# Hybrid decoder trunk: order of the fourth head's products and split of the last head's gating in the matrix-memory layer

## The reference

```
s   = (q k^T) * exp(d - m)                  # scores times decays
num = w_inter * (q C) + s v                 # per head, 256 value features
qn  = w_inter * (q n) + sum(s)
h   = num / max(|qn|, exp(-m))
C   = w_old * C + sum(w_s * k v^T)          # the state, carried from block to block
y   = (sigmoid(o) * h) @ w_out              # gate, then the output product
```

## Time and profile before

| what | value |
|---|---|
| median of 3 runs | 1314.68 us |
| the profiled execution | 1314.32 us |
| its span (first to last instruction) | 1312.5 us |
| outside the span | 1.8 us |
| granted TensorE clock, mean | 0.999 |
| busy: PE, DVE, ACT, POOL | 99%, 65%, 44%, 5% |
| recurrence and start of the output product | about 171 to 206 us of the span |

### The profile page before, as it was taken

How to read it: one execution, slowest core, us unless ns; L and a number is a source line. 1 busy time by engine, 2 the same in 40 slices (tenths; PEclk the granted TensorE clock), 3 DMA queues, 4 the chain that set the end, 5 groups by cost and what they waited for, 6 DMA issues and landing times.

```text
span 1312.5 us, 25501 instructions
## 1 busy us (share of the span) xinstructions
PE 1304.9 (99%) x10940; PEld 1270.3 (97%) x10940; DVE 856.1 (65%) x1554; ACT 583.2 (44%) x1033; POOL 68.0 (5%) x104
## 2 busy tenths in 40 slices
PE   9999999999999999999999999999999999999998
PEld 8999989999999999999999987999999999999998
DVE  6437676887777775222887788698777777432385
ACT  5222354654444443222755768554444444322371
POOL 1110331000000000000012010000000000000000
PEclk9999999999999999999999999999999999999999
DMA  5543732223233234222414232221232233322231
GB/s 176 168 108 99 239 113 79 84 66 96 84 95 97 84 95 134 89 89 83 145 33 160 83 98 79 83 79 42 91 97 92 86 98 105 116 89 89 77 130 66
DMA packets 35089, 131.64 MB, mean 100 GB/s; under 512 B 4228, under 2 KB 4812, under 8 KB 34688
## 3 DMA queue, kind: packets, MB, share of 16 engines
q1 hardware_dynamic: 29520, 111.33, 26.5%
q0 software_dynamic: 5024, 18.05, 4.4%
q10 hardware_dynamic: 432, 0.64, 0.2%
HBM read 121.08 MB, written 10.05 MB: 100 GB/s over the span
## 4 chain that ended last, share of the span: by engine, by line
PE 96%; DVE 2%; ACT 2%; issue 0%; POOL 0%; DVEq 0%; ACTq 0%; POOLq 0%
PE tile L1159 24%; PE tile L1161 24%; PE tile L1163 24%; PE tile L1169 4%; PE tile L1170 4%; PE tile L1171 4%; PE tile L1674 1%; PE side L1169 1%; PE side L1170 1%; PE side L1171 1%; DVE wL L1857 0%; PE side L1289 0%; ACT xH L768 0%; PE side L1334 0%; ACT wH L741 0%
## 5 line engine op out<-in xcount | busy, mean ns | idle before, releaser
L741 ACT ACTIVATE wH<-raw 128x1024 fp32r<-128x1024 f32 (+1 forms) x190 | 210.7, 1112 | 381.1 <-DMA raw<-in_w_up 149.1
L1159 PE MATMUL tile<-xH,wH 128*128 128x260 f32 x1800 | 364.4, 283 | 0.0
L1163 PE MATMUL tile<-xH,wL 128*128 128x260 f32 x1800 | 362.7, 283 | 0.0
L1161 PE MATMUL tile<-xL,wH 128*128 128x260 f32 x1800 | 362.2, 283 | 0.0
L1857 DVE TENSOR_TENSOR wL<-raw,wH 128x1024 fp32r<-128x1024 f32 (+1 forms) x190 | 246.1, 1296 | 154.4 <-ACT wH L741 150.2
L1159 PEld LDWEIGHTS tile<-xH,wH 128*128 128x128 f32 x1800 | 277.3, 189 | 3.2 <-DVE kvq L1905 2.6
L1163 PEld LDWEIGHTS tile<-xH,wL 128*128 128x128 f32 x1800 | 277.5, 188 | 0.0
L1161 PEld LDWEIGHTS tile<-xL,wH 128*128 128x128 f32 x1800 | 276.8, 188 | 0.0
L1905 DVE SCALAR_TENSOR_TENSOR u<-tile,rstd 128x520 f32<-128x520 f32 x96 | 67.1, 699 | 122.8 <-PE tile L1163 122.7
L1159 PE MATMUL tile<-hidH,wH 128*128 128x260 f32 x616 | 124.3, 283 | 0.0
L1163 PE MATMUL tile<-hidH,wL 128*128 128x260 f32 x616 | 123.8, 282 | 0.0
(11 more groups left out here) (462 smaller groups left out, 1895.8 us busy)
## 6 DMA issues: line engine op xcount, KB each, us to landing
raw<-in_w_up SPq DMA_DIRECT2D x88, 512.0 KB, 3.6
raw<-in_w_down SPq DMA_DIRECT2D x32, 704.0 KB, 4.1
raw<-in_w_ple SPq DMA_DIRECT2D x16, 512.0 KB, 5.3
raw<-in_w_qo SPq DMA_DIRECT2D x12, 512.0 KB, 3.6
raw<-in_w_qkv SPq DMA_DIRECT2D x12, 512.0 KB, 3.6
raw<-in_w_kv SPq DMA_DIRECT2D x10, 512.0 KB, 3.6
cring<-in_c_in POOLq DMA_DIRECT2D x8, 512.0 KB, 4.5
out_c_s<-cring POOLq DMA_DIRECT2D x8, 512.0 KB, 3.6
```

The source lines that it names most:

```text
L741: nc.scalar.activation(wH[j][:, 0:n], raw[j][:, 0:n], ACT.Copy).then_inc(s_high, 1)
L1159: nc.tensor.matmul(out[:, q, 0:HT], wh, x[0][:, k, tokens(q)], start=first, stop=False)
L1161: nc.tensor.matmul(out[:, q, 0:HT], wh, x[1][:, k, tokens(q)], start=False, stop=False)
L1163: mm = nc.tensor.matmul(out[:, q, 0:HT], wl, x[0][:, k, tokens(q)], start=False, stop=last)
```

## The change

Three edits. PE does `scores(3)` ahead of `outer(1, 2, NB)` and `values(1)`, no longer behind them. The last of the last head's four numerators is divided by DVE (`last_numerator`), directly behind `denominators(3)`, instead of by ACT. `gated(3)` raises a semaphore of its own after its first half, on which ACT starts the first of the last head's two roundings, and it stands ahead of `clear_acc()`.

```diff
+        s_gated0 = sem("last_head_half_gated")
...
             def numerators(n):
-                for b in range(NB):
+                for b in range(NB - 1 if n == NH - 1 else NB):
...
             def x_high(n):
-                act.wait_ge(s_afin, n + 2)
+                if n == NH - 1:
+                    act.wait_ge(s_gated0, 1)
+                else:
+                    act.wait_ge(s_afin, n + 2)
                 for k in (2 * n, 2 * n + 1):
+                    if k == 2 * NH - 1:
+                        act.wait_ge(s_afin, NH + 1)
                     nc.scalar.activation(xH[:, k, :], o_tile(k), ACT.Copy).then_inc(s_xh, 1)
...
+            scores(3)
             outer(1, 2, NB)
             values(1)
-            scores(3)
             turn_numerators(0)
...
                     last = nc.vector.tensor_tensor(o, side[:, half, :], o, ALU.mult)
+                    if half == 0 and n == NH - 1:
+                        last.then_inc(s_gated0, 1)
                 last.then_inc(s_afin, 1)
+
+            def last_numerator():
+                n, b = NH - 1, NB - 1
+                at0 = NB * (n % 2) + b
+                dve.wait_ge(s_den, 2 * NH)
+                nc.vector.tensor_scalar(ytok[n % 2][:, b, :], num_bank(b)[:, 0:DV], rden[:, at0:at0 + 1], None, ALU.mult
+                                        ).then_inc(s_nr, 1)
...
             denominators(3)
+            last_numerator()
             low("mout", 2)
+            gated(3)
             clear_acc()
-            gated(3)
             dve.wait_ge(s_xr, XSET["mout"] + 2 * (NH - 1))
             o_low(NH - 1)
```

## The result

The changed kernel takes **1317.97 us** (median of 15 runs, 1316.30 to 1319.60), the kernel before beside it 1314.53 (15 runs, 1314.17 to 1315.36): a ratio of 1.0025 [1.0018, 1.0032] (the bracket is the 95% interval), 3.44 us **slower**. The prediction was 1314.2, no change, in a range that ended at 1315.0. It was wrong.

A forecast was written before the change was run, and what follows sets the result against it. PE, busy 99% of the span, bounds the kernel; only its idle time could be gained. Early gains were lost waiting for POOL's k = 5, leaving 0.48 us at k = 7: 1314.68 - 0.48 = 1314.2 us, range 1313.4 to 1315.0.

The forecast's parts named there:

- edit 2: Last numerator divided by DVE: `low` starts 0.49 later, `turn_numerators(3)` loads 0.82 earlier including the earlier gain of 0.45.
- rival 3: Slower: POOL runs k = 4 and k = 5 before `low`; PE's k = 7 1.3 late, 1316.0 us; chance 0.09.
- decision point: On DVE, `low` starts after POOL's k = 4 only if `last_numerator` takes over 0.6 us.
- edit 1: `scores(3)` moved ahead on PE: `outer(2, 0)` 0.50 earlier, 0.45 us taken as gained, bounds 0.28 and 0.50.
- the tight wait at `outer(2, 2)`: PE's `outer(2, 2)` needs ACT's numerators of head 1, ready at 187.44; up to 0.1 us given back.
- edit 3: Half gating, `clear_acc` later: memset falls inside the wait for POOL, semaphore costs nothing, k = 7 loads at 204.43.
- Rival 2: No gain: POOL's k = 4 first by a little, `low` waits, k = 7 0.1 later, 1314.8 us; chance 0.15.
- About 0.2% ... none of the cases reaches that: About 0.2%, or 2.6 us, is what measurement can tell from no change; no case was said to reach it.
- The four waits: PE's late starts at 181.45, 200.35, 204.36 and 204.91: 0.40, 0.46, 0.33 and 0.19 us, together about 1.3.

The follow-up runs named there:

- e2: Changed kernel with `scores(3)` back behind `values(1)`, so only the moved division, half gating and later memset remain: 1317.29 us against 1314.49 before.
- e4: Changed kernel with POOL's scaling of head 2's queries made to wait for the sample outputs' last step: 1316.69 us against 1314.49 before.
- e5: Changed kernel with 18 additional, unused matmuls on PE ahead of its wait for k = 6: 1316.14 us against 1314.62 before.
- e10: Changed kernel with a tiny DVE memset between `last_numerator` and `low`: 1317.80 us against 1314.47 before.
- e12: Changed kernel with a 4-column memset on POOL, and a wait for it, between k = 4 and k = 5: 1315.39 us against 1314.48 before.
- e11: Changed kernel with a 4-column memset on POOL, and a wait for it, ahead of k = 4: 1314.81 us against 1314.47 before.
- e9: Changed kernel with a 256-column memset on POOL, and a wait for it, ahead of k = 4: 1314.92 us against 1314.47 before.
- e1: Kernel before with only `scores(3)` moved ahead of `outer(1, 2, NB)`: 1314.70 us against 1314.49.
- e8: Kernel before with only half gating of the last head and `clear_acc()` behind `gated(3)`: 1314.12 us against 1314.62.
- e7: Kernel before with `clear_acc()` moved ahead of `low` on DVE: 1314.62 us against 1314.62.
- e6: Changed kernel with `low` moved into `states(1)` and POOL's scaling of head 2's queries behind the sample outputs: 1313.22 us against 1314.62 before.

## Why the prediction was wrong

**The step that failed most: edit 2, "`low` lies at 199.28 to 200.49".** All the working behind it took a lead of 0.17 over POOL for a won race. The lead came out as foreseen (0.15), and the race was lost, to both tiles. What happened is rival 3, to which 0.09 was given and which the range left out: POOL first with k = 4 and with k = 5, `low` after them, then `gated(3)`, `x_high` and k = 6 and 7. Its decision point ("if `last_numerator` takes over 0.6 us") was wrong: the new instruction took 0.48, inside its bounds, and was enough. Recorded leads in these runs, all with POOL's k = 4 as the other side: behind the division 0.15 to 0.17 lost (after, e2, e4, e5, e10, e12), 0.34 and 0.57 won (e11, e9); behind the reciprocal 0.66 to 0.70 won (before, e1, e8); behind the big memset 0.13 won (e7). Counting from the recorded end of DVE's instruction ahead of `low` sorts them no better: leads of 0.07 to 0.09 lost (after, e2, e4, e5, e10, e12), 0.05 won (e7). For a recorded lead within 0.2 us both outcomes should have had a fair chance, and 1316 should have been in the range.

The Trainium skill, "SBUF — State Buffer", section "SBUF: two separate sides", says that of a VectorE instruction with two SBUF inputs and a GpSimd instruction that reads SBUF, whichever starts first has the shared ports for its whole length; its section "Who interferes with whom" says: "Issue order, not op shape, decides who blocks." The runs agree on the holding: whichever lost ended 1.1 to 1.2 us after the other had (`low` in the changed kernel and e12, k = 4 in e7, e8 and e11), nearly its own length. They differ from the plain reading of it: the order of the starts in the trace is not that order, since `low`, recorded 0.15 earlier, lost.

**Rival 3's price was too small**: +1.3 at k = 7; it was +1.93. That miss is edit 1's, below: rival 3 counted on edit 1's 0.45, and where edit 1 does gain (e4), k = 7 is only 1.10 late. The larger miss is behind k = 7: PE's idle 2.05 us were followed by 3.3 us at 1.2 GHz, worth 1.4 to 1.8 (e5; 1.50 by the distances). No step of the prediction had the clock.

**Edit 1, "I take 0.45 gained", failed too.** It was a loss of 0.22 at `outer(2, 0)`. The prediction looked for waits behind the delayed instructions, but not at which of them meets POOL, and it counted the query scaling among the delayed, which it wasn't: the sample outputs' last step, delayed with the rest, came just behind the scaling and took 1.07 instead of 0.23. It also left out that `turn_numerators(0)` waits for that step. With that order put right (e4, e6) the gain is 0.55, close to the 0.50 that was worked out; the tight wait at `outer(2, 2)` cost nothing that shows.

**Right:** `low` holds POOL and the memset doesn't (e7, e8); k = 4 ends 1.17 after `low`; PE would wait some 0.8 at k = 5 if `low` were first (0.90 in e9 and e11); edit 3 costs nothing and gains by itself (0.38 at k = 7, e8). Rival 2 was the right kind of doubt (POOL "first by a little") with one tile too few. "About 0.2% ... none of the cases reaches that" fell with rival 3's price. The four waits that the prediction lists add up to 1.38 us, not 1.3; nothing hangs on it.

## What to carry to other kernels

Before delaying a VectorE instruction that reads two SBUF operands, list what GpSimd runs within a microsecond of it, and count a lead of a few tenths as a race that may be lost, to everything queued back to back on GpSimd. The cure here was not to make it faster but to put it where GpSimd is idle, or to let GpSimd wait for a short one. And where a change can leave TensorE idle for 2 us, price the slower clock that may follow as well as the wait.

## What was not expected of the hardware

- **A waiting VectorE instruction isn't let in between two back-to-back GpSimd tiles**: 3.83 us beside k = 4 and k = 5, but 2.56 with a memset of 0.09 us and a wait for it between them (e12).
- **The order of recorded starts doesn't tell which of two engines goes first** when they are this close. Behind the division the point lies between leads of 0.17 (lost) and 0.34 (won); behind the big memset 0.13 was enough (e7), behind a tiny one 0.15 was not (e10). What moves it was not settled.
- **PE's clock could fall after 2 us without a matmul, at no fixed distance from them**: granted 0.50 some 1 us after work had resumed in the changed kernel (207.3 to 210.7), 0.3 after in e4 (from 206.3), just before it in e10 (from 206.1, work from 206.2), and not at all in e2. The times and mean clocks of the changed kernel's runs fit a fall in twelve of 15; only the profiled one shows it. What decides it was not settled.
